# The second layer's first four tiles prepared inside the first layer's output stage

## The reference

```
mod_x = split(silu(c) @ w_ada[l] + b_ada[l])           # shift, scale, gate; mod_c the same from c_ctx
xn = rmsnorm(x, norm_g) * (1 + scale_x) + shift_x      # start of layer l
cn = rmsnorm(ctx, norm_g) * (1 + scale_c) + shift_c
aq, ak, av, az, mq, mk, mv, mo, mz, mi, mf = project(xn, w_in)   # the same for cn
...  # window attention (att_x) and a chunked mLSTM with a gated head norm (m_x)
out_x = concat([att_x, m_x]) @ w_out                   # end of layer l
x = x + gate_x * out_x
```

## Time and profile before

| | us |
|---|---|
| median of 3 runs | 2917.93 (2916.2 to 2919.82) |
| the profiled execution | 2912.02 |
| its span, first to last instruction | 2910.3 |
| PE busy | 2732.0 (94%) |
| DVE busy | 1570.8 (54%) |
| ACT busy | 987.0 (34%) |
| POOL busy | 295.6 (10%) |
| mean granted TensorE clock | 0.971 |

### The profile page before, as it was taken

One profiled execution on the slowest core, in us unless ns is written; L12 is line 12 of the kernel. 1 busy time (PEld: TensorE's weight loads), 2 busy tenths in 40 slices (PEclk: granted clock), 3 DMA queues, 4 the chain that ended last, 5 costly groups with the idle time before them and its releaser, 6 DMA issues. The chain is left out here.

```text
span 2910.3 us, 38758 instructions
## 1 busy us (share of the span) xinstructions
PE 2732.0 (94%) x15704; PEld 2262.7 (78%) x15704; DVE 1570.8 (54%) x2475; ACT 987.0 (34%) x1832; POOL 295.6 (10%) x258
## 2 busy tenths in 40 slices
PE   6999999999987899999989879998999999999998
PEld 3789888779765699887778658865688888888887
DVE  4312575778542612776767544969834444444445
ACT  3201233555521411234546334268622112112112
POOL 0000101211431000101204410000100000000001
PEclk8999999999998899999989989999999999999999
DMA  6322322015454222321044431100300101101112
GB/s 269 94 83 80 84 82 73 16 37 200 142 209 166 103 76 80 94 84 50 16 166 135 146 129 38 46 15 1 138 15 30 58 31 56 58 34 52 58 38 84
DMA packets 111560, 244.89 MB, mean 84 GB/s; under 512 B 10963, under 2 KB 66181, under 8 KB 103089
## 3 DMA queue, kind: packets, MB, share of 16 engines
q1 hardware_dynamic: 90256, 228.03, 23.0%
q10 hardware_dynamic: 21152, 14.75, 1.6%
HBM read 194.51 MB, written 42.99 MB: 82 GB/s over the span
## 5 line engine op out<-in xcount | busy, mean ns | idle before, releaser
L921 PE MATMUL ps<-xn_hi_sb,ft_hi_sb 128*128 128x512 f32 (+1 forms) x720 | 263.8, 366 | 1.0 <-DVE ft_lo_sb L1343 1.0
L922 PE MATMUL ps<-xn_lo_sb,ft_hi_sb 128*128 128x512 f32 (+1 forms) x720 | 263.0, 365 | 0.0
L923 PE MATMUL ps<-xn_hi_sb,ft_lo_sb 128*128 128x512 f32 (+1 forms) x720 | 262.6, 365 | 0.0
L2976 DVE TENSOR_TENSOR arena_sb<-arena_sb,ps 128x512 f32<-128x512 f32 x256 | 172.8, 686 | 121.6 <-PE ps L2655 118.9
L869 PE MATMUL ps<-tm_hi_sb,xn_hi_sb 128*128 128x512 f32 (+2 forms) x608 | 215.7, 355 | 0.8 <-DVE xn_lo_sb L1270 0.8
L871 PE MATMUL ps<-tm_hi_sb,xn_lo_sb 128*128 128x512 f32 (+2 forms) x608 | 213.2, 351 | 0.0
L870 PE MATMUL ps<-tm_lo_sb,xn_hi_sb 128*128 128x512 f32 (+2 forms) x608 | 212.9, 350 | 0.0
L2614 PE MATMUL ps<-xn_hi_sb,w_up_hi_sb 128*128 128x512 f32 x512 | 199.4, 389 | 0.0
L2616 PE MATMUL ps<-xn_hi_sb,w_up_lo_sb 128*128 128x512 f32 x512 | 199.2, 389 | 0.0
L2615 PE MATMUL ps<-xn_lo_sb,w_up_hi_sb 128*128 128x512 f32 x512 | 199.2, 389 | 0.0
L2653 PE MATMUL ps<-w_down_hi_sb,h_hi_sb 128*128 128x512 f32 x480 | 186.7, 389 | 0.0
(11 more groups left out here) (411 smaller groups left out, 6157.7 us busy)
## 6 DMA issues: line engine op xcount, KB each, us to landing
arena_sb<-in_w_ft SPq DMA_DIRECT2D x44, 512.0 KB, 3.6
arena_sb<-mqk_dram SPq DMA_DIRECT2D x36, 512.0 KB, 3.4
arena_sb<-x_dram SPq DMA_DIRECT2D x33, 512.0 KB, 6.6
arena_sb<-in_w_ada SPq DMA_DIRECT2D x16, 1024.0 KB, 8.5
arena_sb<-in_w_up SPq DMA_DIRECT2D x16, 1024.0 KB, 6.5
arena_sb<-in_w_down SPq DMA_DIRECT2D x16, 1024.0 KB, 4.8
arena_sb<-in_xall SPq DMA_DIRECT2D x20, 512.0 KB, 4.7
arena_sb<-mv_dram SPq DMA_DIRECT2D x40, 256.0 KB, 3.9
```

The costliest lines, as they stand in the source:

```text
L921: pe.matmul(to, hi, xn_hi_flat[:, k, at:at + size], start=k == 0, stop=False)
L922: pe.matmul(to, hi, xn_lo_flat[:, k, at:at + size], start=False, stop=False)
L923: mm = pe.matmul(to, lo, xn_hi_flat[:, k, at:at + size], start=False, stop=k == KT - 1)
```

## The change

The semaphores of the norm (`nt_*`), of the first weight block (`tm_w0`, now four) and of the stores (`stored`) are made once for both layers, and counts go on from layer to layer (`tile_no`, `pair_no`). In layer 0's output stage, for layer 1:

- SyncE, behind tile 6's work, waits for all heads (`p_hz`) and for two stores per slot, and loads x tiles 0 to 2 into buffers that the heads used; behind tile 8's store it loads tile 3.
- SyncE, ahead of tile 9's store, waits for the last product and for turn 2 and loads the first weights in four pieces of 512 KB. Only slot 0's stores are awaited at the block's end; slot 1's (tile 9's among them) in layer 1, ahead of block 1's weights.
- TensorE turns tile 0 ahead of product 9, tiles 1 and 2 between its two halves (behind a wait for the gate rows, whose bank is reused), tile 3 behind it. Tiles 0 to 3 use banks 4 to 7.
- VectorE scales tiles 0 to 2 ahead of residual 8, and behind it takes the gate rows, modulates pair 0 and scales tile 3, all ahead of residual 9.
- ScalarE, behind its last gains, squares tiles 0 to 2, copies both banks of tiles 0 to 2, squares tile 3, rounds pair 0 and copies tile 3. GpSimd takes four roots.

In layer 1, VectorE begins with low(0) and the four weight pieces, ScalarE with the four weight pieces and then squares 4 to 6, high(1); TensorE begins with product 0, and turn(t + 4) stands behind product(t). Some buffers move so that these lifetimes fit (`xm`, the second `x_new`, `x_in`, the bias of the late modulation). Cut to its core:

```diff
-        x_new = [part(XL + 4096, D_MODEL), part(ACC + 6144, D_MODEL)]
+        x_new = [[part(XL + 4096, D_MODEL), part(at, D_MODEL)] for at in (CST + 3456, ACC + 6144)]
+        lead_xt = [part(V_TM + 2048 + 1024 * u, D_MODEL) for u in range(3)]
...
# SyncE, norm of layer 1 (load_x of tiles 0 to 3 and the weight halves are gone here)
                 def norm_tm(l):
                     for t in (4, 5):
-                        load_x(t)
+                        load_x(l, t)
+                    if l > 0:
+                        sp.wait_ge(stored[1], 16 * (NTILE // 2))
                     sp.dma_start(tm_raw[1], A["w_tm1"][l]).then_inc(tm_w[1], 16)
# SyncE, output
+                        if leads and t == nt - 1:
+                            sp.wait_ge(p_mm[l], nt)
+                            sp.wait_ge(nt_tr, tile_no(l + 1, 3))
+                            for n in range(4):
+                                load_first_tm(l + 1, n)
                         store(t, t % 2)
...
+                        if leads and t == 6:
+                            sp.wait_ge(p_hz[l], nt)
+                            for u in range(2):
+                                sp.wait_ge(p_store[u], 32)
+                            for n in range(3):
+                                load_x(l + 1, n)
+                        if leads and t == 8:
+                            sp.wait_ge(ada_after["use"], 2 * KT)
+                            load_x(l + 1, 3)
...
-                    for u in range(2):
-                        sp.wait_ge(p_store[l][u], 16 * (nt // 2))
+                    for u in range(2 if l == DEPTH - 1 else 1):
+                        sp.wait_ge(p_store[u], 16 * (nt // 2))
# TensorE, norm
-                        if b == 0 and t + turned_x < NTILE:
-                            turn(t + turned_x)
+                        if l == 0 and b == 0 and t + 4 < NTILE:
+                            turn_x(l, t + 4)
...
                         product(i, b, t)
+                        if l > 0 and b == 0 and t + 4 < NTILE:
+                            turn_x(l, t + 4)
# TensorE, output
                         for c in range(2):
+                            if leads and t == nt - 1 and c == 1:
+                                pe.wait_ge(ada_after["row"], 3)
+                                turn_x(l + 1, 1)
+                                turn_x(l + 1, 2)
...
+                        if leads and t == nt - 1:
+                            pe.wait_ge(p_lo[l], nt)
+                            turn_x(l + 1, 0)
                         product(t, t % 2)
                         modulation(t - 1)
+                    if leads:
+                        turn_x(l + 1, 3)
# VectorE, output
+                        if leads and t == nt - 2:
+                            for n in range(3):
+                                scale_rows(l + 1, n)
                         residual(t, t % 2, gate_x if t < NX else gate_c)
                         if t + 2 < nt:
                             mix_low(t + 2, t % 2)
-                    if l < DEPTH - 1:
-                        gate_rows_of(ada_after, ada_next[2], 6)
+                        if leads and t == nt - 2:
+                            gate_rows_of(ada_after, ada_next[2], 6)
+                            modulate(l + 1, 0)
+                            scale_rows(l + 1, 3)
# VectorE, norm of layer 1
+                    else:
+                        low(0)
+                        for n in range(4):
+                            low_piece(n)
+                        scale_rows(l, 4)
+                        modulate(l, 1)
+                        scale_rows(l, 5)
+                        low(1)
# ScalarE, norm of layer 1
+                    else:
+                        for n in range(4):
+                            high_piece(n)
+                        squares(l, 4)
+                        squares(l, 5)
+                        squares(l, 6)
+                        high(l, 1)
+                        keep(4)
# ScalarE, end of the output
+                    def keep_lead(t):
+                        if t == 0:
+                            act.wait_ge(p_att[l], 2 * nt)
+                        act.wait_ge(nt_tr, tile_no(l + 1, t + 1))
+                        for half, done in enumerate((nt_ev_first, nt_ev_second)):
+                            got = ps[:, turned_bank(l + 1, t) + half, :].rearrange("p (k n) -> p k n", k=4)
+                            act.activation(x_hat[:, 4 * half:4 * half + 4, t, :], got, ACT.Copy).then_inc(done, 1)
+
+                    if leads:
+                        for t in range(3):
+                            squares(l + 1, t)
+                        for t in range(3):
+                            keep_lead(t)
+                        squares(l + 1, 3)
+                        high(l + 1, 0)
+                        keep_lead(3)
```

More of the change, by code:

```diff
@@ L314, in build @@
         xt = [part(TS + 1024 * u, D_MODEL) for u in range(3)]
-        xm = [apart(f"xm{u}", TS + 3072 + 2048 * u, KT, 2 * P) for u in range(2)]
+        xm = [apart(f"xm{u}", at, KT, 2 * P) for u, at in enumerate((ACC + 6144, TS + 5120))]
         x_hat = part(XH, KT, NTILE, P)
@@ L492, in layer_tiles, with tile_no, pair_no, row_at @@
             return NTILE if l < DEPTH - 1 else NX
+        nt_sq, nt_ms, nt_rs, nt_xs, nt_tr, nt_ev_first, nt_ev_second, nt_mod, nt_hi, nt_lo = [nc.alloc_semaphore(name=n) for n in (
+            "nt_sq", "nt_ms", "nt_rs", "nt_xs", "nt_tr", "nt_ev_first", "nt_ev_second", "nt_mod", "nt_hi", "nt_lo")]
+        nt_ld = [nc.alloc_semaphore(name=f"nt_ld{u}") for u in range(3)]
+        tm_w0 = [nc.alloc_semaphore(name=f"tm_w0{n}") for n in range(4)]
+        stored = [nc.alloc_semaphore(name=f"stored{u}") for u in range(2)]
+        def tile_no(of, n):
+            return NTILE * of + n
+        def pair_no(of, n):
+            return NTILE // 2 * of + n
+        def row_at(of, t):
+            return lead_xt[t] if of > 0 and t < 3 else xt[t % 3]
+        def turned_bank(of, t):
+            return 2 * (t % 2) + (4 if of > 0 and t < 4 else 0)
         def first_block_layer(l, block, sems):
+            if l == DEPTH - 1:
+                sems.extend([nt_sq, nt_ms, nt_rs, nt_xs, nt_tr, nt_ev_first, nt_ev_second, nt_mod, nt_hi, nt_lo] + nt_ld + tm_w0 + stored)
             def sem(name):
@@ L1334, in norm_tm @@
                             if t == 0:
-                                dve.wait_ge(gt_zero, 1)
+                                dve.wait_ge(pads[l], 1)
                             evacuate(i, b, t)
@@ L1794, in norm_tm @@
                     evacuate(1, 0)
-                    high(2)
+                    high(l, 2)
                     for p in range(3, NTILE // 2):
                         if 2 * p + 2 < NTILE:
-                            squares(2 * p + 2)
+                            squares(l, 2 * p + 2)
                         keep(2 * p)
@@ L1802, in norm_tm @@
                         if 2 * p + 2 < NTILE:
-                            squares(2 * p + 3)
+                            squares(l, 2 * p + 3)
                         evacuate(2 * p - 3, 0)
-                        high(p)
+                        high(l, p)
                     high_tm(1)
```

235 lines of the change are left out of this document (108 added, 127 removed).

## The result

The changed kernel takes 2895.81 us (median of 4 runs, 2891.12 to 2899.06), the kernel before on the same chip 2917.42 (4 runs, 2916.2 to 2919.82): ratio 0.9924, 95% interval 0.9906 to 0.9941. It is faster by 22 us; 2894.4 was predicted, within 2887 to 2905. The profiled execution took 2891.12 us.

What follows compares the result with a forecast made beforehand. TensorE, busy 94% of the span, bounds; only its 39.0 us hole at the layer seam can pay. 27.9 - 0.4 - 0.9 - 0.5 - 2.7 = 23.4, by dates 23.5; from 2917.93 that gives 2894.4, range 2887 to 2905.

Steps and rivals of the forecast that it cites:

- First product: Start of layer 1's product 0: 934.9 instead of 962.77, 27.9 us earlier.
- slow start: Product 0 at the seam: 7.04 us at the slow clock plus 0.4 for the missing warming turn, to 942.3.
- Product 2's wait: Layer 1, block 0: TensorE there at 949.5, operands through x tile 6 ready at 950.0; new wait 0.5 us.
- Block 1's wait: Layer 1: TensorE ready at 986.2, second weight split done at 988.9 behind turn 9; wait 2.7 us.
- added turns: Layer 0's last output product: three turns at 0.9 us, 2.7 us, so product 9 ends at 926.5 instead of 923.8.
- order of the queue: DMA at the seam: descriptors served in ring order, so x6 stays behind 2 MB of weights, landing about 944.6.
- D: Rival: half clock holds on in layer 1's first products; all eight of block 0 give 2929; chance 0.03.
- A: Rival: slower queue, 6.3 MB at 311 GB/s, product 2 starts 4.3 us later; gain 19.2, 2898.7; chance 0.15.
- B: Rival: block boundary waits for outstanding transfers, block opens at 937.2; gain 18.1, 2899.8; chance 0.10.
- C: Rival: no wait before block 1, turn 9 or copies come sooner; gain 26.2, 2891.7; chance 0.08.
- E: Rival: the change doesn't act, x loads held back to the seam by a store or head wait; 2917.9; chance 0.02.
- terms kept at nothing: Layer 0's four weight pieces 0 (-0.5 to +0.5 us); moved buffers and semaphore clearing each -0.3 to +0.3.

Runs made afterwards that it cites:

- second execution: The changed kernel run again with no edit; 2895.27 us, ratio 0.9938 to the kernel before.
- splits early: Changed kernel with block 1's weights split ahead of the last pair's work in layer 1, that pair's wait moved to block 2; 2890.63 us, ratio 0.9914.
- tile 6 first: Changed kernel with the load of x tile 6 ahead of block 1's 2 MB of weights in layer 1; 2887.35 us, ratio 0.9907.
- two pieces: Changed kernel with layer 0's first weights loaded in two 1 MB halves instead of four pieces; 2894.43 us, ratio 0.993.
- weights late: Changed kernel with layer 1's four first-weight pieces requested when its block opens, not ahead of the last store; 2893.56 us, ratio 0.9932.
- turn 9 early: Changed kernel with tile 9's transposes ahead of product 5, as before the change; 2889.88 us, ratio 0.9915.
- filler in the wait: Changed kernel with ten unused matmuls ahead of TensorE's wait before block 1; 2890.83 us, ratio 0.9924.
- nine fillers: Changed kernel plus early weight splits, x tile 6 ahead of block 1's weights, and unused matmuls: 8 ending layer 0, 9 before product 0; 2886.59 us, ratio 0.9909.

## Why the prediction was right

The steps, each date of the changed kernel with the 1.40 us taken off. The last forecast date is worked out from the recorded ones, 1018.05 less the 23.5 us:

| step | forecast | measured |
|---|---|---|
| store 9 issued | 929.1 | 928.97 |
| block opens | 931.4 | 931.09 |
| product 0 starts | 934.9 | 934.71 |
| turn 4 starts | 942.3 | 942.25 |
| product 2 starts | 950.0 | 950.47 |
| low_tm(1) done, block 1 starts | 988.9 | 989.5, 989.6 |
| first evacuation of block 1 | 994.6 | 996.97 |

**The terms.** First product 27.9 earlier: 28.1. The slow start of 7.4 us: 7.54. Product 2's wait of 0.5: 0.84, 1.2 in the second execution, and up to 1.7 in runs with the same order up to there (splits early). Block 1's wait of 2.7: 2.64. The output stage took its added turns at about the price given (turn 3 starts at 926.2 by that clock, about 926.5 was forecast), and TensorE has no new wait in it. The order of the queue held: the 2 MB, issued at 937.74, landed 7.5 us later, at 945.2, and x tile 6, issued right behind them, at 946.5 (945.1 by that clock; 944.6 was forecast). The Trainium skill (DMA: Bandwidth & Descriptors, section Queues, rings and completion order) states that each DMA engine takes the descriptors of a ring in their order. These landings agree with it. The run with tile 6 first takes the wait away.

**The term that was missing.** A wait of 2.7 us before block 1 was priced at its own length. It also took the clock down: the first product behind it ran 7.3 us instead of the 5.6 of the earlier trace rows (1018.05 less 1012.41), 1.7 us. The prediction had the half clock as a rival (D) only for the long idle time ahead of product 0 and gave a short wait none. That, and 0.7 us of small delays up to there, is the 2.4 us in the last line of the table. By the first evacuation of block 1 the profiled execution is 19.7 us ahead (21.1 without the late layer 0) of the 23.5 forecast; at the end it is 20.9 ahead. On the way the lead moves: 21.3 us at the last of layer 1's feature-major weight loads (1311.3 against 1290.0), 19.5 at the last load for its attention (1572.2, 1552.7), 21.0 at the first of the third layer's (2100.8, 2079.8). What moves it was not followed; none of the moved work stands there.

**The rivals.** A (slower queue): product 2 waits 0.84 us, not 4.8; out. B (boundary waits): out by the changed kernel's own issues and by the run that awaits the store. C (no wait before block 1): out as the kernel stands; with turn 9 moved, the wait is 0.6. D: the clock came back within product 0. E: out, since the three x loads are issued at 890.45 and the turns run inside product 9. Of the terms kept at nothing only the four pieces were run by themselves, and no cost can be seen. The moved buffers and the semaphores were not; the dates up to product 0 lie 0.1 to 0.3 us before the forecast, which leaves them nothing of size up to there.

**The total.** The profiled execution came out 2.6 us above the 2888.5 forecast for it, the median only 1.4 above its own, since it stands 4.7 us over the profiled one and not 5.9: part of the hit is this spread. The gain of 23.5 us itself was forecast a little too large: the two measurements say 22 (17 to 27) and 18 (14 to 22), and in the profiled execution the slow matmuls behind block 1's wait are 1.7 us of what is missing.

## What to carry to other kernels

A long hole between stages is a chain of latencies. Moving the chain's start under the previous stage's products took 31 of its 39 us here, of which about 20 reached the end of the program. Moving the weight request and leaving out the last wait, without the chain, paid nothing, because the request delayed the data behind it in the same queue. After such a move, go through what stands next in order: which load now lies behind a large one, and which split or transpose is now last. A wait of 2 to 3 us on TensorE is to be priced with the slow matmuls that may follow it: here 1.6 us on top of 2.6. Moving one split removed both, and moving one transpose left 0.6 us of the wait.

## What the runs showed of the hardware

- The clock fell behind a 2.6 us idle piece of TensorE in five executions of six with that wait (the changed kernel twice, the last store awaited, two pieces, tile 6 first); in the sixth (weights late) it stayed at 1.00 with the same 2.64 us. What decides between them stays open. It also fell behind a piece of 2.0 us in both runs with fillers ahead of product 0, and not behind 0.6 and 0.4 us (turn 9 early, filler in the wait).
- Behind these short pieces the clock fell only after work had begun again: at 991 to 992 in the changed kernel, at about 934 with nine fillers. In the long hole it fell with TensorE idle: in the changed kernel TensorE stopped at 928.6, the granted clock was 1.00 until 933, 0.75 from 933 to 934 and 0.50 behind. Behind the short pieces it was back 3 to 4 us after the fall.
- A block boundary did not wait for transfers in flight: it opened 2.1 us after a store's issue with the store and two 512 KB loads in flight, and 9.2 us after it where the program awaited the store.
- A 512 KB store behind 2 MB of loads in one queue landed about 7.4 us after its issue (937.74 less 930.37), against 2.6 in the earlier trace rows behind nothing.
